# Transposes of attention probabilities moved behind the second scores, value products one k-step earlier, and ScalarE's normalising copies ahead of its attention copy

## What is computed

```python
s = jnp.einsum('bnqhgd,bnkhd->bnhgqk', qb, kb) * (dh ** -0.5)
s = jnp.where(mask[None, :, None, None], s, -jnp.inf)
m = jnp.maximum(jnp.max(s, axis=-1, keepdims=True), sink)
p = jnp.exp(s - m)
p = p / (jnp.sum(p, axis=-1, keepdims=True) + jnp.exp(sink - m))
o = jnp.einsum('bnhgqk,bnkhd->bnqhgd', p.astype(v.dtype), vb)
y_a = o * jax.nn.silu(gate_a)
y_b = _conformer_conv(u, conv_w[l], conv_b[l], ln_w[l], ln_b[l]) * jax.nn.silu(gate_b)
y = jnp.concatenate([y_a, y_b], axis=-1) @ w_out[l]
```

## Time and profile before

| | us |
|---|---|
| median of 3 runs | 446.83 |
| lowest and highest run | 446.57, 448.25 |
| the profiled execution | 449.1 |
| its span, first to last instruction | 447.4 |
| TensorE busy | 417.6 (93%) |
| VectorE busy | 337.8 (76%) |
| ScalarE busy | 206.6 (46%) |
| GpSimd busy | 123.6 (28%) |

### The profile page before, as it was taken

The page is one execution under the profiler, slowest core; times in us unless marked ns, Lnnn a source line. Parts: engine busy times, 40 slices in busy tenths (PEclk is TensorE's granted clock), DMA queues, the critical chain, the costliest instruction groups (busy, mean ns, idle before and its releaser), DMA issues.

```text
span 447.4 us, 5696 instructions
## 1 busy us (share of the span) xinstructions
PE 417.6 (93%) x2039; PEld 326.9 (73%) x2039; DVE 337.8 (76%) x556; ACT 206.6 (46%) x457; POOL 123.6 (28%) x142
## 2 busy tenths in 40 slices
PE   0779997999999999999999999999799998999997
PEld 0458875887888888767876676687477786888886
DVE  0779768499999989999989797799864998322222
ACT  1636477303502047777777979414324787100000
POOL 1400040001260532354504409943031564100000
PEclk9969999999999999999999999999889999999999
DMA  6999937400890000004012649967245056971111
GB/s 183 327 288 273 367 128 241 136 0 9 239 188 7 6 7 7 9 6 142 1 48 47 122 83 132 172 59 156 33 94 96 0 160 187 261 169 57 58 51 47
DMA packets 62425, 51.39 MB, mean 115 GB/s; under 512 B 19178, under 2 KB 57374, under 8 KB 62397
## 3 DMA queue, kind: packets, MB, share of 16 engines
q1 hardware_dynamic: 46492, 41.59, 31.0%
q0 software_dynamic: 15904, 9.44, 16.1%
HBM read 46.82 MB, written 4.19 MB: 114 GB/s over the span
## 4 chain that ended last, share of the span: by engine, by line
PE 54%; DVE 24%; ACT 4%; issue 3%; POOL 2%; DMA 1%; DVEq 0%; ACTq 0%; POOLq 0%
PE pm L545 6%; PE pm L546 5%; PE pm L547 5%; PE pm L734 4%; PE pm L736 4%; PE pm L735 4%; PE pm L801 3%; PE pm L800 3%; PE pm L802 3%; DVE z L1270 3%; PE ps L669 3%; DVE cacc L1257 2%; PE tr L800 2%; DVE cacc L1250 2%; PE tr L801 2%
## 5 line engine op out<-in xcount | busy, mean ns | idle before, releaser
L545 PE MATMUL pm<-h,wts 128*128 128x512 f32 x224 | 93.1, 416 | 3.5 <-DVE h L1173 2.0
L546 PE MATMUL pm<-h,wts 128*128 128x512 f32 x224 | 88.4, 395 | 0.0
L547 PE MATMUL pm<-h,wts 128*128 128x512 f32 x224 | 88.3, 394 | 0.0
L545 PEld LDWEIGHTS pm<-h,wts 128*128 128x128 f32 x224 | 42.8, 191 | 19.3 <-issue 5.6
L547 PEld LDWEIGHTS pm<-h,wts 128*128 128x128 f32 x224 | 42.7, 191 | 9.3
L546 PEld LDWEIGHTS pm<-h,wts 128*128 128x128 f32 x224 | 42.8, 191 | 8.7 <-issue 1.0
L874 ACT ACTIVATE wts<-raw 128x1024 fp32r<-128x1024 f32 x30 | 31.2, 1051 | 34.7 <-PE pm L547 10.4
L734 PE MATMUL pm<-wts,h 128*128 128x256 f32 (+1 forms) x128 | 45.9, 358 | 0.0
L418 POOL DMA_DIRECT2D wts<-in_w_in x22 | 28.7, 2695 | 62.0 <-ACT wts L876 62.0
L736 PE MATMUL pm<-wts,h 128*128 128x256 f32 (+1 forms) x128 | 43.1, 337 | 0.0
L735 PE MATMUL pm<-wts,h 128*128 128x256 f32 (+1 forms) x128 | 43.1, 336 | 0.0
(11 more groups left out here) (200 smaller groups left out, 908.6 us busy)
## 6 DMA issues: line engine op xcount, KB each, us to landing
raw<-in_w_in SPq DMA_DIRECT2D x18, 512.0 KB, 6.6
slab<-in_w_ada SPq DMA_DIRECT2D x16, 512.0 KB, 7.3
xs<-in_x SPq DMA_DIRECT2D x8, 512.0 KB, 7.4
raw<-in_w_ada SPq DMA_DIRECT2D x8, 512.0 KB, 4.6
xr<-in_x SPq DMA_DIRECT2D x8, 512.0 KB, 4.4
out<-xr SPq DMA_DIRECT2D x15, 256.0 KB, 2.2
wts<-in_w_in POOLq DMA_DIRECT2D x6, 512.0 KB, 7.8
raw<-in_w_in SPq DMA_DIRECT2D x16, 128.0 KB, 2.8
```

What stands on the lines that cost most here:

```text
L545: pe.matmul(out, hi_w, hi_x, start=first, stop=False)
L546: pe.matmul(out, lo_w, hi_x, start=False, stop=False)
L547: return pe.matmul(out, hi_w, lo_x, start=False, stop=last)
```

## The change

`transpose_p` goes from s = 0 of step b + 4 to s = 12 of step b + 3, directly behind the second scores. `times_v` goes from s = 6 to s = 5 of step b + 4, directly behind the transposes of queries and keys. On ScalarE `normalize` comes ahead of `copy_att` (and, in step 11, of two tanh copies, where there is nothing left to normalise). No instruction is added, taken away or made another size.

```diff
             def attention_step(n, s):
-                new, old = n - 2, n - 4
-                if 0 <= old < NT:
-                    if s == 0:
-                        transpose_p(old)
-                    if s == 6:
-                        times_v(old)
+                new, mid, old = n - 2, n - 3, n - 4
                 if 0 <= new < NT:
                     if s == 5:
                         transpose_qk(new)
...
                     if s == 12:
                         scores(new, 1)
+                if 0 <= mid < NT and s == 12:
+                    transpose_p(mid)
+                if 0 <= old < NT and s == 5:
+                    times_v(old)
...
+                if 0 <= b3 < NT:
+                    normalize(b3)
                 if 0 <= b4 < NT:
                     copy_att(b4)
                 if n == 11:
                     tanh_gate(2, 0)
                     tanh_gate(2, 1)
-                if 0 <= b3 < NT:
-                    normalize(b3)
```

## The result

| | before | changed |
|---|---|---|
| median, 20 runs each | 448.77 us | 452.47 us |
| profiled execution | 449.1 us | 452.79 us |
| its span | 447.4 us | 451.1 us |
| ratio changed/before | | 1.0067, 95% interval 1.0041 to 1.0094 |

The kernel before is slower here than in the three runs shown ahead of the prediction, which are the first three of these 20: 448.77 in place of 446.83.

What follows compares the result with a forecast made beforehand. TensorE was taken to bound the kernel until about 265 us, then ScalarE, GpSimd and VectorE. The sum 0.50 + 0.40 + 0.40 + 1.05 + 0.65 = 3.00 us, carried to the median, gave 449.8 us, range 447.1 to 451.7.

Steps and rivals of the forecast that it cites:

- the last of the sum: Whole kernel: 3.00 us added to the profiled 449.1, then the 2.3 us difference carried to the median 446.83, giving 449.8.
- the clock in the tail: Rival behind L752: a shorter TensorE pause keeps the clock up, giving 448.6 or 447.1 us; chance 0.17.
- Stalls in front of the transposes: Steps 3 to 7: without cover, transposes wait for ScalarE's normalising copies, 0.72, 0.34, 0.40, 0.40 and 1.33 us.
- What they leave on the path: Steps 3 to 7: lag from the transposes' stalls, 0.50 for steps 3 and 4, then 0.40, 0.40 and 1.05 us.
- Step 4's wait for VectorE: Second scores of step 4: the 0.56 us wait for VectorE's previous-key copy swallows 0.56 of step 3's 0.72 us stall.
- pairs save their 0.1 us: Smaller-lag rival, steps 3 to 9: paired neighbours save 0.1 us each, or waits swallow stalls; 447.8 to 448.6 us; chance 0.17.
- Value products: Steps 9 and 10: one k-step less ahead of GpSimd's masks, costing 0.65 us in step 9 and 0 in step 10.
- The path behind step 9: Second scores, ScalarE copies, masks, GpSimd's DMA issues, last masks, VectorE's convolution: resumes 3.0 us after 284.98.
- The pause in front of the channel mean: TensorE's wait at L752 for VectorE's channel sum: 1.9 to 2.3 us in place of 2.6.
- The clock did not fall in the stalls: Judges a rival: the clock falls in the new stalls, around step 7, costing about 1.5 us, 451.3 us; chance 0.10.
- Pairing: Rival: each pair of neighbours saves a whole break of 0.36 us in the main matmuls, 5.4 us, giving 444.4; chance 0.06.
- the earlier place gives nothing back: Steps 4 to 10: earlier transposes let ScalarE copy probabilities sooner, but other waits and GpSimd's DMA issues leave a gain of 0.

Runs made afterwards that it cites:

- the later runs: Both kernels measured once more, unchanged: the kernel before against itself 1.0020, the changed kernel 1.0037 against the kernel before.
- the cover given back: Against the kernel before: transposes of probabilities at s = 15 of the same step, ScalarE's swap, value products at s = 6; ratio 0.9989.
- the transposes alone: Against the kernel before: only the transposes moved behind the second scores, value products at s = 6, ScalarE's order old; ratio 1.0078.
- The delay in step 5: Kernel before with one k-step issued four times at the head of step 5, 2.04 us of extra TensorE work; ratio 1.0046.
- the same in step 12: Kernel before with the same 2.04 us of extra TensorE work at the head of step 12; ratio 0.9982.
- the kernel with the masks earlier: Against the kernel before: transposes earlier where covered, ScalarE's swap, transposed probabilities copied ahead of weight copies, step 11's value products at s = 2, step 7's weight copy earlier; 0.9945.
- the two kernels with masks earlier: First the kernel with the masks earlier, 0.9945; second the same plus two extra k-steps (1.36 us) in front of L752, 0.9932, both against the kernel before.
- the four with a shorter pause or none: Kernel before with 2.04 us extra in step 12 (0.9982) or one k-step ahead of L752 (0.9969), and the two kernels with masks earlier (0.9945, 0.9932).

## Why the prediction was right and wrong

The forecast was a lag of 3.00 us (0.7%) and a time of 449.8 us in a range of 447.1 to 451.7. The measured ratio is 1.0067, the measured time 452.47, outside the range. That the ratio agrees so closely is partly luck: the middle gives 2.64 us, or 1.0059, and the two measurements, 1.0067 and 1.0037, scatter around that.

**The step that failed is the last of the sum: the level that the difference was carried to.** I added 3.0 to 446.83, the median of three runs, and took that for the level of the kernel. Twenty runs put it at 448.77, and 448.77 + 3.0 = 451.8, already outside the range by 0.1. The other 0.7 us of the 452.47 the change does not account for: the two medians differ by 3.70 us, of which the middle explains 2.64, and in the later runs they differed by 1.4 (450.15 against 448.76). The sum against the profiled execution, 449.1 + 3.0 = 452.1, before I carried it to the median, came within 0.7 of the profiled 452.79. The range had room for the unknown costs of the change and for the clock in the tail, all in the form of differences, but none for the level. The three runs shown, 446.57 to 448.25, and the profiled execution at 449.1 already spanned 2.5 us, nearly the range's lower half of 2.7. The profiles show where the scatter lies: about 1 us ahead of the attention, its cause open, and 3 us between the channel mean and L767, by the granted clock. I had named that clock as something that the change might move, when it scatters from one execution of the same kernel to the next.

**Stalls in front of the transposes.** Expected 0.72, 0.34, 0.40, 0.40 and 1.33 us in steps 3 to 7; the view has 0.65, 0.32, 0.33, 0.33 and 1.28. Counted as in the prediction, from 1.06 us behind the start of the second scores, they are 0.72, 0.40, 0.41, 0.41 and 1.35. The cause is shown by the cover given back (no stall, middle as before) and the size by the transposes alone.

**What they leave on the path.** Expected 0.50 + 0.40 + 0.40 + 1.05 = 2.35. The first scores of consecutive steps moved apart by 0.39 over steps 3 and 4, then 0.34, 0.34 and 0.93 (for step 6: 228.71 - 213.97 = 14.74 changed, 226.85 - 212.45 = 14.40 before), 2.0 in all. Step 4's wait for VectorE swallowed its part as reckoned. Steps 5 to 7 each came out 0.06 to 0.12 us cheaper than forecast, though their stalls were as long as forecast: the small side of "pairs save their 0.1 us", if the new neighbours are the cause, which no run shows by itself.

**Value products.** Expected 0.65 for step 9 and 0 for step 10; alone they gave 0.82 in the middle, in the changed kernel 0.68 between the first scores of steps 8 and 9 (262.16 - 244.39 = 17.77 against 17.09). The stall of step 10, 0.97 us, did not reach the end, as reckoned. The sum for the middle, 3.00, was 0.36 too high.

**The path behind step 9.** VectorE's convolution resumed 288.47 - 284.98 = 3.49 us later, of which 0.79 came from the head: 2.70. The delay in step 5 against the same in step 12 shows that a lag of TensorE counts in full ahead of step 9 and hardly at all in step 12.

**The pause in front of the channel mean** was to shrink to 1.9 to 2.3 us and is 2.57. Part of TensorE's extra lag, 0.4 us, went into waits for banks that VectorE's gates free: 0.7 us in two before, 0.3 in one now. The rest I did not trace.

**The rivals.** The clock did not fall in the stalls: the window from 173 to 246 us of the changed kernel has a granted clock of 1.00. Pairing gave about 0.1 us a step at most, not 0.36. That the earlier place gives nothing back was right for this change, in which ScalarE's weight copies stayed in front of the copies of transposed probabilities; the kernel with the masks earlier, which turns that order round among other moves, gained 2.7 us.

## What to carry to other kernels

A transfer of work to an earlier place in an in-order engine is worth what waits for it and costs what used to cover its own wait: read the end of its producer and the end of the instruction in front of the new place, and the difference is the stall. Compare executions by a stretch between two fixed events, here repeated to 0.03 us while whole executions scatter by several, and put the scatter of the level into a range for an absolute time, not only the doubts about the change. Before moving work earlier, look for what else stands between it and its reader; here four weight copies on ScalarE stood there, and a kernel that also went around them came out faster than both.

## What the runs showed that I had not expected

**GpSimd and VectorE hold each other up.** In the two kernels with masks earlier the masks behind GpSimd's eight issues run beside VectorE's convolution. In the first, VectorE's multiply-adds of 0.74 us took 1.12 and GpSimd's masks 0.97 to 1.18 in place of 0.64:

```profile
279.48 1.12 DVE L1252 SCALAR_TENSOR_TENSOR z<-z,cw 128x512 f32<-128x512 f32 x1
...
278.87 1.18 POOL L455 TENSOR_SCALAR_AFFINE_SELECT pprev<-pcur 128x512 f32<-128x512 f32 x1 [0.44 <-ACT pcur L964]
```

In the second, with the same instructions there, the first mask took 3.83 us while VectorE kept its 0.75, until VectorE had to wait for the masks, for 2.53 us:

```profile
277.94 3.83 POOL L455 TENSOR_SCALAR_AFFINE_SELECT pprev<-pcur 128x512 f32<-128x512 f32 x1 [0.45 <-ACT pcur L969]
...
283.81 0.76 DVE L1264 SCALAR_TENSOR_TENSOR z<-z,cw 128x513 f32<-128x513 f32 x1 [2.53 <-POOL pcur L459]
```

That is the 1.1 us by which its middle is longer: 2.53 us of waiting in place of four multiply-adds each 0.38 us slower, 1.5 us. In the kernel before VectorE stood waiting when these masks ran, and they took 0.63 to 0.77 us. But the first pattern is there too, in step 9: its last mask took 0.97 us beside

```profile
254.61 1.12 DVE L1270 SCALAR_TENSOR_TENSOR z<-z,cws 128x512 f32<-128x512 f32 x1
```

The Trainium skill, "SBUF — State Buffer", section "SBUF: two separate sides", says that VectorE instructions with two inputs in SBUF and GpSimd instructions that read SBUF contend for one pair of ports as an exclusive lock: whichever starts first has it for the whole instruction, and the other blocks fully. The second kernel agrees in that one mask was held up, to 3.83 us, across several multiply-adds. The first does not look like it in whole: both engines went on, VectorE's instructions slower by 0.38 us and GpSimd's by 0.3 to 0.5, as if they took turns. The start does not tell the two apart: in both kernels the first mask starts 0.06 us behind a multiply-add (278.87 against 278.81, and 277.94 against 277.88). Which of the two patterns comes I can't say.

**The clock behind the channel mean.** The same instructions between L752 and L767 took 18.1 to 21.4 us, by whether and where the granted clock fell. The two profiles of the changed kernel have 21.4 and 18.6, those of the kernel before 21.1 and 20.6, and the four with a shorter pause or none 18.2 to 19.8. Neither the change nor the pause alone sets it; what does stays open.
